# S5 layer of a decoder step: where the rotated states are kept and scanned, and when the first table is begun

## The reference, cut to what matters

```
u   = xn.reshape(b, t, 64 groups, 16)
a_bar = exp(a * dt)                                  # 64 groups x 64 states, complex
bu  = einsum('gnc,btgc->btgn', b_bar, u)             # input to each state
h[t] = a_bar * h[t-1] + bu[t]                        # the scan over time
y   = Re(einsum('gcn,btgn->btgc', c, h)) + d_skip*u
y   = gelu(y);  out = y * sigmoid(y @ w_glu + b_glu)
state = h at the last token (prompt) / after one token (samples)
```

## Time and profile before

| what | value |
|---|---|
| median of 3 runs | 1651.81 us |
| lowest, highest | 1646.07, 1661.41 us |
| profiled execution, its own time | 1661.28 us |
| its span, first to last instruction | 1659.6 us |
| mean granted TensorE clock | 0.963 |
| TensorE busy | 1568.6 us |
| VectorE busy | 885.0 us |
| GpSimd busy | 285.3 us |

### The profile page before, as it was taken

One profiled execution on the slowest core, in us unless ns is written; L12 is line 12 of the kernel. 1 busy time (PEld: TensorE's weight loads), 2 busy tenths in 40 slices (PEclk: granted clock), 3 DMA queues, 4 the chain that ended last, 5 costly groups with the idle time before them and its releaser, 6 DMA issues. The chain is left out here.

```text
span 1659.6 us, 23929 instructions
## 1 busy us (share of the span) xinstructions
PE 1568.6 (95%) x8773; PEld 1220.3 (74%) x8773; DVE 885.0 (53%) x2004; ACT 445.5 (27%) x1107; POOL 285.3 (17%) x365
## 2 busy tenths in 40 slices
PE   7999999989998789999899999988999999999997
PEld 6843676664545368888788888868788888888886
DVE  2312223258884447955456673477057555766514
ACT  3001122258884204333330000133252111100001
POOL 0000210000004312799600001738000000000000
PEclk9999779989999899999999999999999999999998
DMA  5119233312004972455434342060221221322301
GB/s 186 51 63 256 68 95 112 102 32 72 1 1 157 348 220 95 147 191 172 147 127 127 124 130 83 26 280 17 93 102 51 102 100 53 126 77 78 101 26 52
DMA packets 140118, 182.16 MB, mean 110 GB/s; under 512 B 30826, under 2 KB 99250, under 8 KB 138978
## 3 DMA queue, kind: packets, MB, share of 16 engines
q1 hardware_dynamic: 136194, 170.15, 31.2%
q0 software_dynamic: 3808, 10.49, 1.9%
HBM read 163.49 MB, written 29.69 MB: 116 GB/s over the span
## 5 line engine op out<-in xcount | busy, mean ns | idle before, releaser
L291 PE MATMUL psum<-xT,l_w 128*128 128x260 f32 x384 | 88.5, 392 | 4.9 <-PEq L116 3.4
L937 PE MATMUL psum<-xT,l_w 128*128 128x260 f32 x384 | 88.8, 394 | 2.6 <-PEq L116 2.6
L1924 PE MATMUL psum<-cmp_xt,cmp_w 64*128 64x256 f32 (+2 forms) x640 | 88.0, 407 | 2.4
L291 PEld LDWEIGHTS psum<-xT,l_w 128*128 128x128 f32 x384 | 74.8, 195 | 17.7 <-issue 5.0
L937 PEld LDWEIGHTS psum<-xT,l_w 128*128 128x128 f32 x384 | 75.6, 197 | 15.1 <-issue 2.7
L1611 PE MATMUL psum<-proj_w,xT 128*128 128x512 f32 x192 | 86.4, 609 | 0.0
L953 PE MATMUL psum<-l_up_t,l_w_sums 128*128 128x260 f32 x336 | 78.2, 382 | 0.0
L1924 PEld LDWEIGHTS psum<-cmp_xt,cmp_w 64*128 64x128 f32 x640 | 60.8, 215 | 18.7 <-issue 16.0
L2310 ACT ACTIVATE att_p<-att_p,att_low 128x512 f32<-128x512 f32 (+3 forms) x128 | 70.9, 557 | 9.7 <-DVE att_low L2247 9.3
L1611 PEld LDWEIGHTS psum<-proj_w,xT 128*128 128x128 f32 x192 | 36.9, 195 | 48.7 <-issue 48.7
L953 PEld LDWEIGHTS psum<-l_up_t,l_w_sums 128*128 128x128 f32 x336 | 63.8, 190 | 9.8
(11 more groups left out here) (547 smaller groups left out, 3261.1 us busy)
## 6 DMA issues: line engine op xcount, KB each, us to landing
l_w<-in_mlp_w SPq DMA_DIRECT2D x16, 2048.0 KB, 8.6
l_w<-in_mlp_w SPq DMA_DIRECT2D x32, 1024.0 KB, 5.2
proj_w<-in_nsa_w_in SPq DMA_DIRECT2D x4, 2048.0 KB, 9.1
cmp_raw<-in_cache_kv_cmp SPq DMA_DIRECT2D x32, 256.0 KB, 3.0
xT<-in_cache_kv_cmp SPq DMA_DIRECT2D x32, 256.0 KB, 3.1
sa_more<-in_cache_kv_sel POOLq DMA_DIRECT2D x52, 128.0 KB, 7.6
sa_more<-in_cache_kv_sel SPq DMA_DIRECT2D x44, 128.0 KB, 8.9
l_w<-in_nsa_w_o SPq DMA_DIRECT2D x2, 2048.0 KB, 12.9
```

The source lines that it names most:

```text
L291: mm = nc.tensor.matmul(ps[:, n % 8, 0:HALF], w[s][:, k, m * P:(m + 1) * P], src[:, kk, cols(h)], start=(kk == 0), stop=(kk == last))
L937: mm = nc.tensor.matmul(ps[:, n % 8, 0:HALF], w[s][:, k, m * P:(m + 1) * P], src[:, kk, cols(h)], start=(kk == 0), stop=(kk == last))
L1924: mm = nc.tensor.matmul(ps[:, 3 + i % 2 * 2 + z, 0:n], w1[z * HD:(z + 1) * HD, i % 2, t].rearrange("p r e -> p (r e)"), xt[z * HD:(z + 1) ...
```

## The change

There are three edits. (1) The rotated states don't go to the SBUF tile `t1`: `read` first makes the two sine products in `t2`, then multiplies the PSUM banks in place by the cosine; `scan` adds and subtracts from PSUM and `t2` back to PSUM (in a packed layout in the same banks) and scans from there. The banks are thus needed until the scan's end, and TensorE's five waits for a free bank are on `scanned` in place of `x_read`; `last_states` waits for both. (2) GpSimd doesn't copy the last column of each tile, but those of all tiles in two instructions behind the last one, with a semaphore of their own, `fin_kept`. (3) The wait ahead of the first table is for 12 of the 16 increments of `x_ready`.

```diff
-            tables.pool(pool, lambda eng: eng.wait_ge(x_ready, 2 * KD), lambda eng: eng.wait_ge(step_done, 7 * STEPS))
+            tables.pool(pool, lambda eng: eng.wait_ge(x_ready, 2 * KD - 4), lambda eng: eng.wait_ge(step_done, 7 * STEPS))
...
+        self.hxs = c.vt_all[:].rearrange("p k i q x -> p k (i q x)")[:, :, 0:2 * QK * (YCOLS + 1)].rearrange("p k (i q x) -> p k i q x", i=2, q=QK)
...
-        self.t1 = c.causal[:, 0:2 * QK * NCH].rearrange("p (i x) -> p i x", i=2)
...
 turn_z:             if k in (3, 5, 4, 6):
-                pe.wait_ge(self.x_read, k - 2)
+                pe.wait_ge(self.scanned, k - 2)
 states_in:          elif k == 6:
-                pe.wait_ge(self.x_read, 6)
+                pe.wait_ge(self.scanned, 6)
 chunk_outputs:      elif k == 3:
-                pe.wait_ge(self.x_read, 7)
+                pe.wait_ge(self.scanned, 7)
 turn_y:             if k == 0:
-                pe.wait_ge(self.x_read, 5)
+                pe.wait_ge(self.scanned, 5)
 last_states:        pe.wait_ge(self.x_read, KD)
+            pe.wait_ge(self.scanned, KD)
...
             if n == 4:
-                pe.wait_ge(self.turned_back, KD)
+                pe.wait_ge(self.fin_kept, 2)
...
 read:               for i in range(2):
-                nc.vector.tensor_mul(four(t1[:, i]), x[:, i, :, 0:NCH], rot[:, 0, qs]).then_inc(self.x_mixed, 1)
                 nc.vector.tensor_mul(four(t2[:, i]), x[:, 1 - i, :, 0:NCH], rot[:, 1, qs]).then_inc(self.x_mixed, 1)
+            dve.wait_ge(self.x_mixed, 6 * k + 2)
+            for i in range(2):
+                nc.vector.tensor_mul(x[:, i, :, 0:NCH], x[:, i, :, 0:NCH], rot[:, 0, qs]).then_inc(self.x_mixed, 1)
             nc.vector.tensor_add(xs[:, :, qs], xs[:, :, qs], x[:, :, :, NCH:]).then_inc(self.x_read, 1)
 scan:
+            x = ps[:, S[k]:S[k] + 2, 0:QK * YCOLS].rearrange("p i (q x) -> p i q x", q=QK)[:, :, :, 0:NCH]
             dve.wait_ge(self.x_mixed, 6 * k + 4)
-            nc.vector.tensor_add(t1[:, 0], t1[:, 0], t2[:, 0]).then_inc(self.x_mixed, 1)
-            nc.vector.tensor_sub(t1[:, 1], t1[:, 1], t2[:, 1]).then_inc(self.x_mixed, 1)
+            dve.wait_ge(self.x_read, k + 1)
+            packed = ps[:, S[k]:S[k] + 2, 0:QK * NCH]
+            nc.vector.tensor_add(four(packed[:, 0]), x[:, 0], four(t2[:, 0])).then_inc(self.x_mixed, 1)
+            nc.vector.tensor_sub(four(packed[:, 1]), x[:, 1], four(t2[:, 1])).then_inc(self.x_mixed, 1)
...
-                ins = nc.vector.tensor_tensor_scan(self.gs[:, k % 2, i, :], self.rt[:, k], t1[:, i, :], 0.0, ALU.mult, ALU.add)
+                ins = nc.vector.tensor_tensor_scan(self.gs[:, k % 2, i, :], self.rt[:, k], packed[:, i], 0.0, ALU.mult, ALU.add)
...
-            ve.tensor_copy(self.fin[:, :, qs], h[:, :, :, YCOLS]).then_inc(self.turned_back, 1)
+            pool.sem_inc(self.turned_back, 1)
+        for i in range(2):
+            ve.tensor_copy(self.fin[:, i].rearrange("p (k q) -> p k q", q=QK), self.hxs[:, :, i, :, YCOLS]).then_inc(self.fin_kept, 1)
```

More of the change, by code:

```diff
@@ L3227, in __init__ @@
         self.x_mixed, self.ah_ready, self.rho_rows_ready = (c.sem(f"ss_{x}") for x in ("x_mixed", "ah_ready", "rho_rows_ready"))
-        self.h_late, self.h_ready = c.sem("ss_h_late"), c.sem("ss_h_ready")
+        self.h_late, self.h_ready, self.fin_kept = c.sem("ss_h_late"), c.sem("ss_h_ready"), c.sem("ss_last_kept")
+        self.hxs = c.vt_all[:].rearrange("p k i q x -> p k (i q x)")[:, :, 0:2 * QK * (YCOLS + 1)].rearrange("p k (i q x) -> p k i q x", i=2, q=QK)
         self.ut = at("ut", [P, G, XCOLS], 0)
@@ L3531, in dve @@
         c, nc, ps, rot, rs = self.c, self.c.nc, self.c.psum, self.c.rot, self.rs
-        t1, t2, xs = self.t1, self.t2, self.xs
+        t2, xs = self.t2, self.xs
         Z = (2, 4, 2, 6, 4, 2, 6, 6)
```

## The result

| what | before | after |
|---|---|---|
| median of 20 runs each | 1651.57 us | 1667.77 us |
| lowest, highest | 1644.75, 1664.72 | 1652.60, 1671.80 |
| profiled execution, its span | 1661.28, 1659.6 | 1653.13, 1651.5 |
| mean granted TensorE clock in it | 0.963 | 0.973 |
| ratio after to before | | 1.0055, 95% interval 1.0028 to 1.0082 |

The change made the kernel slower by about 9 us (4.6 to 13.5 by the interval). I had forecast 1651 us, and 1664 as the upper end.

A forecast was written before the change was run, and what follows sets the result against it. TensorE, busy 95% of the span, was taken as the bound. Edits 1, 2 and 3 summed as -0.4 + 0 + 0 = -0.4 us on the profiled 1661.28, carried to the median 1651.81: 1651 us, range 1642 to 1664.

The forecast's parts named there:

- 1.33 us for each held operation: Tables: spacing forecast for eleven two-input SBUF operations on VectorE, each waiting for one GpSimd operation.
- 9.0 us late on VectorE: Tables: delay forecast for VectorE's last sum of squares, from the held operations.
- a cover of 4.2 us: Tables: slack from the last input sum (692.12) to its product (696.34), leaving TensorE 4.8 us late.
- late by less, inside this: Tables: `x_ready` and TensorE's sum of the squares were taken as covered by TensorE's 4.8 us delay.
- GpSimd is ready by then: Last table: GpSimd ready near 813, before TensorE, 4.8 us late, comes to it at 816.6.
- the waits go: Last two tables: TensorE's waits, 4.8 us together, vanish, but the same time stands 130 us earlier: 0.0.
- scan 4 ends 4 x 4.66 later: Recurrence: VectorE tiles of 4.66 us put scan 4's end at 1131.8, four tiles after scan 0's at 1113.2.
- 4.64, so it keeps pace: Recurrence: without the copy GpSimd needs 4.64 us a tile, against VectorE's 4.66.
- (a): Rival, tables come free: VectorE gets in more often or slack hides it; edit 3 -5.9, total 1645.5; chance 0.20.
- (b): Rival, VectorE's joins held longer than 1.33 us; at 1.70 sum +5.4, 1657; loss from about 1.4; chance 0.18.
- (c): Rival, recurrence: PSUM doesn't free the scan, or it is slower from there; edit 1 +5.3, 1657; chance 0.12.
- (d): Rival: both (b) and (c) hold, in tables and recurrence, giving 1662; chance 0.03.

The follow-up runs named there:

- e3: e1 with the second sum of squares in PSUM bank 3 instead of 0, its wait moved to the fourth product; tables' stretch 162.66 us.
- e6: e3 with the first table's wait for 14 increments instead of 12; tables' stretch 161.71 us, before 161.66.
- e5: Edits 1 and 2 alone, plus `state_outputs(0)` ahead of `turn_z(5)` and `turn_z(7)` ahead of `turn_y(0)`; `states_in(6)` at 28.84 us, recurrence 60.16.
- e8: Before with edits 1 and 2, e5's TensorE order and the last two tables taken later, without the early table; ratio 0.9956 (0.9912 to 0.9999).
- e4: Before with only edit 1's waits on `scanned`, arithmetic still in SBUF; `states_in(6)` at 36.31 us (before 29.59), recurrence 68.63 (before 62.12).
- e1: Before with edit 3 alone; tables' stretch 169.10 us (before 161.66), ratio 1.0011 (0.9966 to 1.0055).

## Why the prediction was wrong

**Edit 3, tables: wrong, 0 forecast, +7.1 measured.** The contention itself was sized well: 1.33 us for each held operation against 1.24 to 1.45 measured; 9.0 us late on VectorE forecast, 8.4 measured at the read of the squares (687.93 before, 682.63 after, less the anchors). This is what the Trainium skill says (SBUF — State Buffer, "SBUF: two separate sides"): of two sharers of the port pair the later one waits for a whole operation. The trace agrees, with 1.24 to 1.45 us beside GpSimd for what takes 0.34 alone.

Step that failed first: "a cover of 4.2 us". I measured the cover at the last input sum, which the fifth product needs (696.34), and set aside "`x_ready` and TensorE's sum of the squares" as "late by less, inside this". But the read of that sum frees the bank of the *first* product, and there the cover was 689.33 - 687.93 = 1.4 us. 8.4 less 1.4 is 7.0, the shift of that product; the low clock behind it added 2.2, where I had put 1.1. e3 takes out just this wait and gets 5.1 us back up to the last table; there the wait I had named appears, 2.4 us.

Step that failed second: "GpSimd is ready by then", so "the waits go". One of the two went. I followed GpSimd only through its own operations. What it waits for were also TensorE's taking of the first table and the store of the second, both paced by the late first pair. The store's cover was at most small in before as well: issued at 714.29, with up to 13.0 us to land, for a table that started at 729.15. And in e6, without these waits, a lead of 1.8 us was gone by the seventh table all the same.

**Edit 1, recurrence: mechanism right but for one wait, -0.4 forecast, +1.1 measured.** Scans of 1.26, tiles of 4.6 to 4.7 and TensorE's waits on the scan all came as written, and no PSUM price was seen: 0.42 to 0.43 us for the addition and subtraction. The estimate from the Trainium skill's figures for a PSUM source (VectorE: DVE Perf Modes, "The TRN2 errata") was +1.0, close to the total, but by a cause that the rows exclude. Up to the end of scan 3 the forecast held to 0.1 us (18.55 us behind the first `read`). The step that failed is "scan 4 ends 4 x 4.66 later": it assumes that VectorE never waits for TensorE. It waited 0.88 us for it, and 0.46 ahead of scan 4, so scan 4 ended 24.35 us behind the first `read` instead of 23.2; another 0.3 came behind it. The 0.46 isn't TensorE's doing: it stands ahead of scan 4 in all four traces with edit 1, in e5 and e8 too, where `read(4)` waits for nothing. Its cause is open. The added hold delays `turn_z(5)`, and `states_in(4)` is queued behind it: the prediction lists what is queued behind the waits, but follows only the last one. e4 and e5 show both: the hold alone costs 6.7, and order takes 1.8 back (30.67 to 28.84; 2.2 in e8).

**Edit 2, copies: right as far as seen, never run alone.** GpSimd has six operations fewer (365 to 359), and no wait of TensorE in the recurrence is ended by it. "4.64, so it keeps pace" was a little low: where it isn't waiting, a tile of GpSimd takes 4.79 to 4.80 us, more than VectorE's 4.68, because without the copy it waits 0.15 us for its own result. Nothing waited for it.

**Rivals.** (a), free tables, is excluded by 169 us in two traces. (b) had the right sign and place on VectorE, but not the right price: from 658.10 to 670.31 nine held operations took 1.36 us each on the mean, under the 1.4 from which (b) sees a loss, and still it was slower. What decided was the consumer. (c), and (d) with it, is excluded by the scans. The median of 1667.77 lies above my range, 16.2 over before's, where the stages give 8.2 and the ratio 9. What puts the rest into the median is not shown by any stage that the edits touch, and stays open.

## What to carry to other kernels

When an edit delays an engine, list every consumer of every instruction behind it in its queue, with its own slack, and not only the last of the chain: an instruction of 0.4 us that frees a PSUM bank can have the least. A head start is worth only the slack of the producer's own waits, for slots and for stores; where the consumer waits at a few known places, moving the consumer later was the cheaper repair. Where an edit lengthens the hold of a buffer, look at the consumer's order in the same step, since work that doesn't need the buffer may stand behind the wait.

## What was unexpected in the hardware

- A two-input VectorE operation with one operand in PSUM escapes GpSimd's interference, and this holds for the scan too: 1.26 us for two with GpSimd working, against 2.05 from SBUF.
- GpSimd isn't spared when VectorE's queue is full of short SBUF operations: its first operation took 1.69 us in after and 2.37 in e6, against 1.11 in before. The prediction had put this cost at next to nothing.
- A wait of TensorE can cost more than itself. Behind 6.26 us of idle time 16 matmuls took 5.83 us instead of 3.67; behind 2.84 us, 16 others took 3.48 instead of 1.97. The length of the wait alone doesn't decide it: behind 1.42 us (after, 1126.70) and 1.94 us (before) `state_outputs` took its usual 1.97, behind 1.68 us it took 3.64, and in e1, with the same code, 1.97 behind 1.66.
